# Head norm sums of two attentions, gathered into batches that sit side by side in the columns of the TensorE array

## The chip, the cores and the metric

The kernel runs on one core of one Trainium2 chip, as one program. The metric is the device time of one execution in microseconds (us); lower is better. The core has five engines that matter here, each with its own instruction stream, in order, tied to the others only by semaphores: TensorE (PE, matmuls into the accumulation memory `ps`), VectorE (DVE), ScalarE (ACT), GpSimd (POOL), and SyncE (SP), which issues the DMAs that bring the weights in.

## The reference, cut to what matters

A first block (a state-space mixer, a convolution and a product-key expert layer) is followed by a second block of two transformer layers with four feed-forward parts. The change touches the attention of each of these two layers, and in it the root-mean-square norm of the heads:

```python
def _rms_norm(x, g=None, eps=1e-6):
    y = x * rsqrt(mean(x * x, axis=-1) + eps);  return y * g

# first attention: 8 heads x 2 halves of 64 numbers, for q and for k: 32 sums for each of 272 tokens
q = _rms_norm(q.reshape(bsz, t, 8, 2, 64), qk_norm[0])
k = _rms_norm(k.reshape(bsz, t, 8, 2, 64), qk_norm[1])
...
# second attention: 16 heads of 256 numbers, q alone: 16 sums for each of 256 tokens
q_abs = _rms_norm(q_abs.reshape(bsz, t, 16, 256), q_norm)
```

All data are float32. There are T = 272 tokens (16 of them meta tokens, META; the other 256 are SEQ), the model is D = 1024 = 8 x 128 wide (KD = 8), HEADS = 16, P = 128.

## The kernel before, in words

**Layout and weights.** Activations lie transposed: 128 features on the partitions, the tokens along the free dimension. A weight matrix comes as units of 128 x 1024 float32 (512 KB) into a ring of four slots. For each unit ScalarE makes a high part (`w_hi`, L432), VectorE the rest (`ring_lo`, L438), and TensorE's `split` (L548 to L550) forms the product from three matmuls for each of eight 128 x 128 blocks: high by high, high by low, low by high, so 24 matmuls of 272 columns a unit. A slot is free for the next DMA when TensorE has done its unit (`unit_done`).

**First attention, projection (`a_in`).** Units 0 to 7 give q (two half-heads of 64 rows in each), 8 to 15 give k, 16 to 23 give v. TensorE runs `straight` for unit e; VectorE scales the result out of `ps` (`scale_unit`, L1781) and then makes `ring_lo` of unit e + 2 (`low_ahead`); ScalarE makes `w_hi` of unit e + 2 and then the squares of unit e into `sq[:, e % 8]` (L2307, signal `qk_sq`). The mean over the 64 rows of each half is a matmul: `qk_square_sum(i)` (L919) multiplies the squares of unit i by 32 columns of `pair_mean`, which holds 1/64 in two columns and zeros elsewhere, its window shifted so that the two sums of unit i fall in rows 2i and 2i + 1 of 32 rows of bank 5. The sixteen of them add up in one accumulation. Sum e - 1 follows unit e on TensorE; the last one follows `v_unit(0)`. These are plain float32 matmuls, which the trace records as two passes each.

**What uses the sums.** ScalarE takes the root of the 32 rows (L2310), VectorE the reciprocal (L1856), and `spread_qk(i)` (L945) copies the row pair of unit i out to 128 rows with a matmul against `pair_rows`, 32 rows deep; VectorE's `norm_qk` (L1796) applies it, and the logits follow (`a_logits`, L956).

**Second attention.** Nine units of the up-projection (`up_q(j)`, L1123 to L1125, 256 columns a matmul) give first the index queries and then the sixteen heads, two heads a unit, two 128-row blocks a head. ScalarE squares each block (L2439), GpSimd adds the two blocks of a head (L2611, signal `qa_pair`), and `q_square_sum(hd)` (L1156) sums them with `q_mean` into row hd of bank 4: two after each unit, four after the last. In the same stretch VectorE selects the keys (L1969, L1971: eight rounds of maximum and replace) and makes `ring_lo` of the next units between the rounds. Then ScalarE takes the root (L2460), TensorE turns it (`turn_roots`, L1169), VectorE takes the reciprocal (L1986), and `b_start` uses one column of it for each head.

**Two places whose form is like the change's.** In the state-space mixer of the first block, `mix_step` (L715, L717) makes float32 matmuls of 64 columns whose results go by turns to rows 0 to 63 and 64 to 127 of one bank: for each of four heads two matmuls, so two tiles of the array by turns. In `a_logits` (L956) the two halves m = 0 and m = 1 of a head use rows 0 to 63 and 64 to 127 of the array, each matmul again two passes, and write to two banks.

**The constants.** GpSimd writes `pair_mean`, `q_mean` and `pair_rows` at the start of the first feed-forward part (L2590 to L2599).

Of the kernel before, what the change touches and what calls it, by code (L numbers as in the profile page):

```python
# [14 lines left out]
P = 128  # L15
# [106 lines left out]
def build(nc, a, out):  # L122
# [3 lines left out]
    with ExitStack() as ctx:  # L126
# [209 lines left out]
        meta_t = m3(KD, META)  # L336
        pair_mean = m3(1, 4 * HEADS - 2)[:, 0, :]
        head_mean = m3(1, 2 * KD - 1)[:, 0, :]
        pair_rows = m3(2 * HEADS, 64)
        m3.at = GATED_AT + 2 * (FF_CHUNKS + KD) * T + 2 * KD * 8 + 3 * D  # L340
        q_mean = m3(1, 2 * HEADS - 1)[:, 0, :]
        q_inv = m3(1, SEQ)
# [13 lines left out]
        top8 = m3(1, 16)  # L356
        small_b = m3(1, 64)
        g_b = m3(1, 2)
# [166 lines left out]
        def _(pe):  # L525
# [389 lines left out]

            def qk_square_sum(i):

                pe.wait_ge(qk_sq, i + 1)
                nc.tensor.matmul(ps[0:2 * HEADS, 5, 0:T], pair_mean[:, 2 * (HEADS - 1 - i):2 * (HEADS - 1 - i) + 2 * HEADS],  # L919
                                 sq[:, i % 8, :], start=i == 0, stop=i == HEADS - 1).then_inc(head_stat, 1)  # L920

# [16 lines left out]
            def spread_qk(i):  # L938

                hd, part = i // 2, i % 2  # L940
                if i >= 3:
                    pe.wait_ge(qk_ready, i - 2)
                row = 2 * (KD * part + hd)
                rows = pair_rows[0:2 * HEADS, row:row + 2, :].rearrange("p a n -> p (a n)")
                nc.tensor.matmul(ps[:, 5 + i % 3, 0:T], rows, qk_inv[0:2 * HEADS, 0, :],  # L945
                                 start=True, stop=True).then_inc(head_spread, 1)
# [74 lines left out]
            for e in range(16):  # L1021
                straight("a_in", e, normed(0), T, normed_before=None if e else 8 * NORM["a"])
                if e == 0:
                    summed_stats("a", 0)
                    pe.wait_ge(means_made, 2)
                else:
                    qk_square_sum(e - 1)
            v_unit(0)
            qk_square_sum(15)
            pe.wait_ge(acc_free, OUT0["a_in"] + 15)  # L1030
# [119 lines left out]

            def q_square_sum(hd):

                pe.wait_ge(qa_pair, hd + 1)
                if hd == 0:
                    pe.wait_ge(lat_std, 3)
                nc.tensor.matmul(ps[0:HEADS, 4, 0:SEQ], q_mean[:, HEADS - 1 - hd:2 * HEADS - 1 - hd], sq[:, 2 * hd % 8, 0:SEQ],  # L1156
                                 start=hd == 0, stop=hd == HEADS - 1).then_inc(qa_stat, 1)

            for j in range(2, 10):
                if j < 9:  # L1160
                    up_q(j)
                q_square_sum(2 * (j - 2))
                q_square_sum(2 * (j - 2) + 1)

            def turn_roots():

                pe.wait_ge(head_root, 3)
                for t in range(2):
                    last = nc.tensor.transpose(ps[:, 5, TILE_W + t * HEADS:TILE_W + (t + 1) * HEADS],  # L1169
                                               q_inv[0:HEADS, 0, t * P:(t + 1) * P], ident[0:HEADS, 0:HEADS])  # L1170
                last.then_inc(head_spread, 1)
# [77 lines left out]
        def _(dve):  # L1249
# [605 lines left out]
            dve.wait_ge(head_root, 1)  # L1855
            V_.reciprocal(qk_inv[0:2 * HEADS, 0, :], qk_inv[0:2 * HEADS, 0, :]).then_inc(head_inverse, 1)  # L1856
            scale_unit(17)
# [125 lines left out]
            sb_ = small_b[:, 0, :]  # L1983
            inv = sb_[:, 16:16 + 2 * HEADS]
            dve.wait_ge(head_spread, HEADS + KD + 1)
            link(V_.reciprocal(inv, ps[:, 5, TILE_W:TILE_W + 2 * HEADS]))  # L1986

            def b_start(hd):
                dve.wait_ge(b_logits, hd + 1)
                dve.wait_ge(sel_added, hd + 1)  # L1990
                if hd >= 2:
                    dve.wait_ge(b_turned, 2 * (hd - 1))
                c = 8 * (hd % 2)
                for t, (a0, a1) in enumerate(TILES):
                    ins = V_.scalar_tensor_tensor(soft_b[:, hd % 2, a0:a1], ps[:, hd % 4, a0:a1], inv[:, t * HEADS + hd:t * HEADS + hd + 1],
                                                  bias[:, hd, a0:a1], ALU.mult, ALU.add)
# [35 lines left out]
        def _(act):  # L2032
# [276 lines left out]
            act.wait_ge(head_stat, 16)  # L2309
            A_(qk_inv[0:2 * HEADS, 0, :], ps[0:2 * HEADS, 5, 0:T], ACT.Sqrt, bias=eps[EPS_2][0:2 * HEADS]).then_inc(head_root, 1)  # L2310
            act.wait_ge(lam_mm, 1)
# [147 lines left out]
            act.wait_ge(qa_stat, HEADS)  # L2459
            A_(q_inv[0:HEADS, 0, :], ps[0:HEADS, 4, 0:SEQ], ACT.Sqrt, bias=eps[EPS_2][0:HEADS]).then_inc(head_root, 1)  # L2460
            def value_part(i):
# [53 lines left out]
        def _(pool):  # L2515
# [78 lines left out]
            for half in range(2):  # L2594
                at_col = 2 * (HEADS - 1) + half
                nc.gpsimd.tensor_copy(pair_mean[:, at_col:at_col + 1], C("mean_64")[:, 64 * half:64 * half + 1])
            nc.gpsimd.tensor_copy(pair_rows[0:2 * HEADS, :, :], bc(ident[0:2 * HEADS, 0:2 * HEADS], 2, 64))
            nc.gpsimd.tensor_copy(q_mean[:, HEADS - 1:HEADS], C("mean_256", 1))
            nc.gpsimd.tensor_copy(head_mean[:, KD - 1:KD], C("mean_128", 1)).then_inc(means_made, 1)  # L2599
# [106 lines left out]
```

## Time and profile before

| what | value |
|---|---|
| median of 3 runs | 2277.86 us (2277.47 to 2278.12) |
| span of the profiled execution | 2276.2 us |
| rest of the median beyond that span | 1.66 us |
| PE busy | 2198.8 us (97%) |
| DVE busy | 1609.5 us (71%) |
| ACT busy | 1195.7 us (53%) |
| POOL busy | 319.0 us (14%) |
| DMA, mean over the span | 158 GB/s |

The span runs from the first to the last instruction of one profiled execution; only this span is known of that execution, and the median of the unprofiled runs lies 1.66 us above it. A busy share is an average over stages: 97% says that TensorE nearly always has something in it, not that each of its instructions is on the path that sets the end. Matmul records overlap, since they are pipelined; what a matmul costs is read from the distance between starts, not from its duration.

### The profile page before, as it was taken

To read this page: it belongs to the slowest core of one execution; us is meant where nothing else is said; L and a number is where in the kernel's file an instruction comes from. 1 tells how busy PE (TensorE), PEld (TensorE's weight loads), DVE (VectorE), ACT (ScalarE), POOL (GpSimd) and SP (SyncE) were. 2 spreads that over 40 slices of the span, in tenths; PEclk is the share of its full clock that TensorE was granted. 3 is DMA by queue.
4 is the path that set the end of the run, shared out by engine and by line. 5 is a ranking of instruction groups with operands and counts; after the bars stand their busy time and mean duration, and the time that the engine had idled before them with its cause. 6 is when DMAs were issued, how large, how long until landed. Compare 5 with 4: busy or idle time off the path is not lost.

```text
span 2276.2 us, 42952 instructions
## 1 busy us (share of the span) xinstructions
PE 2198.8 (97%) x15644; PEld 2033.2 (89%) x15644; DVE 1609.5 (71%) x2891; ACT 1195.7 (53%) x1739; POOL 319.0 (14%) x220
## 2 busy tenths in 40 slices
PE   7988999999998999999999999999999999999999
PEld 6986899999997788888899998789999999768998
DVE  6797579999859755555687654667667766866764
ACT  5455357777777655555544443634444434764443
POOL 4785100000007300000011000010000001231000
PEclk9999999999999999999999999889999999999999
DMA  4432556666662366666655554135565556304665
GB/s 160 149 103 84 157 185 185 185 185 185 185 179 100 100 188 187 190 186 189 207 176 173 184 167 117 51 102 173 173 183 180 173 173 191 105 26 139 184 181 179
DMA packets 107976, 359.57 MB, mean 158 GB/s; under 512 B 12992, under 2 KB 21568, under 8 KB 107760
## 3 DMA queue, kind: packets, MB, share of 16 engines
q1 hardware_dynamic: 105792, 354.04, 51.8%
q10 hardware_dynamic: 2096, 4.36, 0.6%
q8 instruction: 55, 0.90, 0.2%
q14 instruction: 33, 0.27, 0.0%
HBM read 356.22 MB, written 6.46 MB: 159 GB/s over the span
## 4 chain that ended last, share of the span: by engine, by line
PE 85%; DVE 8%; ACT 2%; POOL 2%; issue 1%; DMA 1%; SPq 0%; ACTq 0%; DVEq 0%; POOLq 0%
PE ps L548 20%; PE ps L550 19%; PE ps L549 19%; PE ps L854 16%; PE ps L786 3%; DVE hot_keys L1643 2%; DVE big L1652 2%; DVE ring_lo L438 1%; PE ps L1184 1%; POOL ring_lo L438 1%; POOL slot_t L2544 1%; ACT w_hi L432 1%; POOL big L2563 0%; PE ps L919 0%; PE ps L1233 0%
## 5 line engine op out<-in xcount | busy, mean ns | idle before, releaser
L432 ACT ACTIVATE w_hi<-ring 128x1024 fp32r<-128x1024 f32 x640 | 676.1, 1057 | 471.0 <-DMA ring<-in_ffn_in_dram 146.4
L438 DVE TENSOR_TENSOR ring_lo<-ring,w_hi 128x1024 fp32r<-128x1024 f32 x600 | 749.8, 1251 | 232.7 <-ACT w_hi L432 228.6
L548 PE MATMUL ps<-hw_hi,w_hi 128*128 128x272 f32 (+1 forms) x3104 | 893.4, 288 | 11.4 <-DVE ring_lo L438 3.0
L550 PE MATMUL ps<-hw_hi,ring_lo 128*128 128x272 f32 (+1 forms) x3104 | 888.7, 286 | 0.0
L549 PE MATMUL ps<-hw_lo,w_hi 128*128 128x272 f32 (+1 forms) x3104 | 887.1, 286 | 0.0
L548 PEld LDWEIGHTS ps<-hw_hi,w_hi 128*128 128x128 f32 x3104 | 589.0, 190 | 24.8 <-issue 8.8
L550 PEld LDWEIGHTS ps<-hw_hi,ring_lo 128*128 128x128 f32 x3104 | 589.3, 190 | 0.0
L549 PEld LDWEIGHTS ps<-hw_lo,w_hi 128*128 128x128 f32 x3104 | 587.7, 189 | 0.1
L854 PE MATMUL ps<-w_hi,hid_parts 128*128 128x512 f32 x1024 | 279.7, 395 | 2.3 <-DVE hid_parts L1671 2.3
L854 PEld LDWEIGHTS ps<-w_hi,hid_parts 128*128 128x128 f32 x1024 | 192.8, 188 | 47.4 <-issue 2.5
L548 PE MATMUL ps<-gated_hi,w_hi 128*128 128x272 f32 (+1 forms) x704 | 201.7, 287 | 3.6 <-DVE big L1738 3.6
L550 PE MATMUL ps<-gated_hi,ring_lo 128*128 128x272 f32 (+1 forms) x704 | 201.2, 286 | 0.0
L549 PE MATMUL ps<-gated_lo,w_hi 128*128 128x272 f32 (+1 forms) x704 | 200.8, 285 | 0.0
L854 PE MATMUL ps<-ring_lo,hid_parts 128*128 128x512 f32 x512 | 160.5, 394 | 0.0
L1738 DVE TENSOR_TENSOR big<-ps,rstd 128x272 f32<-128x272 f32 (+1 forms) x176 | 76.8, 437 | 109.1 <-PE ps L550 104.4
L2576 POOL TENSOR_TENSOR sq<-sq 128x272 f32<-128x272 f32 (+1 forms) x42 | 48.0, 1142 | 743.7 <-ACT sq L2289 478.4
L548 PEld LDWEIGHTS ps<-gated_hi,w_hi 128*128 128x128 f32 x704 | 132.4, 188 | 4.5 <-issue 4.5
L549 PEld LDWEIGHTS ps<-gated_lo,w_hi 128*128 128x128 f32 x704 | 132.5, 188 | 0.0
L550 PEld LDWEIGHTS ps<-gated_hi,ring_lo 128*128 128x128 f32 x704 | 132.3, 188 | 0.0
L854 PEld LDWEIGHTS ps<-ring_lo,hid_parts 128*128 128x128 f32 x512 | 96.5, 188 | 22.6
L2277 ACT ACTIVATE big<-big 128x272 f32<-128x272 f32 (+1 forms) x88 | 37.7, 429 | 146.7 <-DVE big L1738 146.7
L2232 ACT ACTIVATE hid_parts<-big 128x256 fp32r (+1 forms) x128 | 53.4, 418 | 115.1 <-PE ps L854 111.7
(441 smaller groups left out, 2573.8 us busy)
## 6 DMA issues: line engine op xcount, KB each, us to landing
ring<-in_ffn_in_dram SPq DMA_DIRECT2D x176, 512.0 KB, 3.6
ring<-in_down_dram SPq DMA_DIRECT2D x128, 512.0 KB, 4.2
ring<-in_up_dram SPq DMA_DIRECT2D x128, 512.0 KB, 3.6
ring<-in_ffn_out_dram SPq DMA_DIRECT2D x96, 512.0 KB, 3.7
ring<-in_a_in_dram SPq DMA_DIRECT2D x24, 512.0 KB, 3.6
ring<-in_xbc_dram SPq DMA_DIRECT2D x16, 512.0 KB, 3.6
ring<-in_conf_dram SPq DMA_DIRECT2D x16, 512.0 KB, 3.6
ring<-in_mix_out_dram SPq DMA_DIRECT2D x16, 512.0 KB, 3.6
```

The costliest lines, as they stand in the source:

```text
L432: nc.scalar.activation(w_hi[:, u % RING, :], ring[:, u % RING, :], ACT.Copy).then_inc(hi_done, 1)
L438: eng.tensor_tensor(ring_lo[:, u % RING, :], ring[:, u % RING, :], w_hi[:, u % RING, :].bitcast(F32), ALU.subtract).then_inc(split_done, 1)
L548: nc.tensor.matmul(bank_out, w_hi[:, b, w], hi(k0 + k), start=start and k == 0, stop=False)
L549: nc.tensor.matmul(bank_out, w_hi[:, b, w], lo(k0 + k), start=False, stop=False)
L550: last = nc.tensor.matmul(bank_out, ring_lo[:, b, w], hi(k0 + k), start=False, stop=stop and k == m - 1)
L786: last = nc.tensor.matmul(ps[:, (0, 1, 2, 5)[j % 4], (j // 4) * SEQ:(j // 4 + 1) * SEQ], ring[:, u % RING, k * P:(k + 1) * P], mix[:, KD * ...
L854: last = nc.tensor.matmul(ps[:, 2 * t + half, :], hid_parts[:, part, t * P:(t + 1) * P], weight[:, s, half * 512:(half + 1) * 512], start= ...
L1643: V_.tensor_tensor(hot_b[:, n % 2, :, :].rearrange("p t (a k) -> p t a k", k=8), bc(high_digit[:, at_tok:at_tok + 8, :], 3, 8), bc(gate_lo ...
L1652: V_.tensor_tensor(v, v, ps[:, 2 * b:2 * b + 2, :].rearrange("p c (t i) -> p i (c t)", i=P), ALU.mult).then_inc(gated_hid, 1)
L1738: V_.tensor_tensor((up_a, up_b)[s % 2][:, p, c0:T], ps[:, s, 0:T - c0], rstd[:, c0:T], ALU.mult).then_inc(acc_free, 1)
L2232: A_(hid_parts[:, c % PARTS, :], at(hid, it * 4 + c), ACT.Copy).then_inc(hid_hi_done, 1)
L2576: nc.gpsimd.tensor_tensor(sq[:, 0, c0:T], sq[:, 0, c0:T], sq[:, k, c0:T], ALU.add).then_inc(sq_sum, 1)
```

## The change

In the first attention the sixteen sums are no longer made one at a time. `qk_square_sums(b)` makes four in a row, for units 4b to 4b + 3: the sum of unit 4b + g goes to rows 32g to 32g + 31 of bank 5, which is the column quarter g of the array, and within the quarter to its rows 2b and 2b + 1. The batches follow units 4, 8 and 12 and `v_unit(0)`. Root, reciprocal and `spread_qk` now work on 128 rows, not on 32, and `pair_rows` is laid out for that. In the second attention `q_square_sums(p)` makes the two heads of a unit in a row, the first in quarter 0, the second in quarter 1; root and turning work on 64 and 40 rows, the reciprocal on 80 columns in place of 32. The count of matmuls is the same: 16 and 16. Each still signals its own completion.

```diff
-        pair_mean = m3(1, 4 * HEADS - 2)[:, 0, :]
+        pair_mean = m3(1, 38)[:, 0, :]
...
-        q_mean = m3(1, 2 * HEADS - 1)[:, 0, :]
+        q_mean = m3(1, KD - 1 + 32)[:, 0, :]
...
-        small_b = m3(1, 64)
+        small_b = m3(1, 96)
...
-            def qk_square_sum(i):
-
-                pe.wait_ge(qk_sq, i + 1)
-                nc.tensor.matmul(ps[0:2 * HEADS, 5, 0:T], pair_mean[:, 2 * (HEADS - 1 - i):2 * (HEADS - 1 - i) + 2 * HEADS],
-                                 sq[:, i % 8, :], start=i == 0, stop=i == HEADS - 1).then_inc(head_stat, 1)
+            def qk_square_sums(b):
+
+                pe.wait_ge(qk_sq, 4 * b + 4)
+                for g in range(4):
+                    nc.tensor.matmul(ps[32 * g:32 * g + 32, 5, 0:T], pair_mean[:, 6 - 2 * b:38 - 2 * b], sq[:, (4 * b + g) % 8, :],
+                                     start=b == 0, stop=b == 3).then_inc(head_stat, 1)
...
-                rows = pair_rows[0:2 * HEADS, row:row + 2, :].rearrange("p a n -> p (a n)")
-                nc.tensor.matmul(ps[:, 5 + i % 3, 0:T], rows, qk_inv[0:2 * HEADS, 0, :],
+                rows = pair_rows[:, row:row + 2, :].rearrange("p a n -> p (a n)")
+                nc.tensor.matmul(ps[:, 5 + i % 3, 0:T], rows, qk_inv[:, 0, :],
                                  start=True, stop=True).then_inc(head_spread, 1)
...
-                else:
-                    qk_square_sum(e - 1)
+                elif e % 4 == 0:
+                    qk_square_sums(e // 4 - 1)
             v_unit(0)
-            qk_square_sum(15)
+            qk_square_sums(3)
...
-            def q_square_sum(hd):
-
-                pe.wait_ge(qa_pair, hd + 1)
-                if hd == 0:
+            ROOTS = 32 + KD
+
+            def q_square_sums(p):
+
+                pe.wait_ge(qa_pair, 2 * p + 2)
+                if p == 0:
                     pe.wait_ge(lat_std, 3)
-                nc.tensor.matmul(ps[0:HEADS, 4, 0:SEQ], q_mean[:, HEADS - 1 - hd:2 * HEADS - 1 - hd], sq[:, 2 * hd % 8, 0:SEQ],
-                                 start=hd == 0, stop=hd == HEADS - 1).then_inc(qa_stat, 1)
+                for m in range(2):
+                    nc.tensor.matmul(ps[32 * m:32 * m + 32, 4, 0:SEQ], q_mean[:, KD - 1 - p:KD - 1 - p + 32],
+                                     sq[:, (4 * p + 2 * m) % 8, 0:SEQ], start=p == 0, stop=p == KD - 1).then_inc(qa_stat, 1)
...
-                q_square_sum(2 * (j - 2))
-                q_square_sum(2 * (j - 2) + 1)
+                q_square_sums(j - 2)
...
-                    last = nc.tensor.transpose(ps[:, 5, TILE_W + t * HEADS:TILE_W + (t + 1) * HEADS],
-                                               q_inv[0:HEADS, 0, t * P:(t + 1) * P], ident[0:HEADS, 0:HEADS])
+                    last = nc.tensor.transpose(ps[:, 5, TILE_W + t * ROOTS:TILE_W + (t + 1) * ROOTS],
+                                               q_inv[0:ROOTS, 0, t * P:(t + 1) * P], ident[0:ROOTS, 0:ROOTS])
...
-            V_.reciprocal(qk_inv[0:2 * HEADS, 0, :], qk_inv[0:2 * HEADS, 0, :]).then_inc(head_inverse, 1)
+            V_.reciprocal(qk_inv[:, 0, :], qk_inv[:, 0, :]).then_inc(head_inverse, 1)
...
-            inv = sb_[:, 16:16 + 2 * HEADS]
+            inv = sb_[:, 16:16 + 2 * (32 + KD)]
             dve.wait_ge(head_spread, HEADS + KD + 1)
-            link(V_.reciprocal(inv, ps[:, 5, TILE_W:TILE_W + 2 * HEADS]))
+            link(V_.reciprocal(inv, ps[:, 5, TILE_W:TILE_W + 2 * (32 + KD)]))
...
-            A_(qk_inv[0:2 * HEADS, 0, :], ps[0:2 * HEADS, 5, 0:T], ACT.Sqrt, bias=eps[EPS_2][0:2 * HEADS]).then_inc(head_root, 1)
+            A_(qk_inv[:, 0, :], ps[:, 5, 0:T], ACT.Sqrt, bias=eps[EPS_2]).then_inc(head_root, 1)
...
-            A_(q_inv[0:HEADS, 0, :], ps[0:HEADS, 4, 0:SEQ], ACT.Sqrt, bias=eps[EPS_2][0:HEADS]).then_inc(head_root, 1)
+            A_(q_inv[0:64, 0, :], ps[0:64, 4, 0:SEQ], ACT.Sqrt, bias=eps[EPS_2][0:64]).then_inc(head_root, 1)
...
-                at_col = 2 * (HEADS - 1) + half
+                at_col = 6 + half
                 nc.gpsimd.tensor_copy(pair_mean[:, at_col:at_col + 1], C("mean_64")[:, 64 * half:64 * half + 1])
-            nc.gpsimd.tensor_copy(pair_rows[0:2 * HEADS, :, :], bc(ident[0:2 * HEADS, 0:2 * HEADS], 2, 64))
-            nc.gpsimd.tensor_copy(q_mean[:, HEADS - 1:HEADS], C("mean_256", 1))
+            for b in range(4):
+                quarter = ident.rearrange("p (g r) -> p g r", r=32)[:, :, 2 * b:2 * b + 2]
+                nc.gpsimd.tensor_copy(pair_rows[:, 8 * b:8 * b + 8, :].rearrange("p (g m) n -> p g m n", m=2), bc(quarter, 3, 64))
+            nc.gpsimd.tensor_copy(q_mean[:, KD - 1:KD], C("mean_256", 1))
```

## Rows read from the trace of the kernel before

**Rows 1.** The page: busy time of TensorE, and the chain that ended last.

```profile
PE 2198.8 (97%) x15644; PEld 2033.2 (89%) x15644; DVE 1609.5 (71%) x2891; ACT 1195.7 (53%) x1739; POOL 319.0 (14%) x220
PE 85%; DVE 8%; ACT 2%; POOL 2%; issue 1%; DMA 1%; SPq 0%; ACTq 0%; DVEq 0%; POOLq 0%
```

**Rows 2.** The first attention's sums by their line: durations, first and last start.

```profile
L919 PE MATMUL ps<-sq,big x32: 392/405/418, 1347.2 to 1404.4; 128*32 128x272 f32 x32
```

**Rows 3.** Timeline of TensorE around one sum: start, length, line, count.

```profile
1358.38 0.29 PE L550 MATMUL ps<-hw_hi,ring_lo 128*128 128x272 f32 x1
1358.60 0.65 PE L919 MATMUL ps<-sq,big 128*32 128x272 f32 x2
...
1359.40 0.29 PE L549 MATMUL ps<-hw_lo,w_hi 128*128 128x272 f32 x1
...
1362.18 0.29 PE L550 MATMUL ps<-hw_hi,ring_lo 128*128 128x272 f32 x1
```

**Rows 4.** Timeline of TensorE in the state-space mixer, matmuls of 64 columns.

```profile
147.67 0.45 PE L715 MATMUL ps<-big 128*64 128x128 f32 x4 [1.02 <-POOL big L2563]
...
148.35 0.44 PE L717 MATMUL ps<-big 128*64 128x128 f32 x4
148.72 0.39 PE L548 MATMUL ps<-hw_hi,w_hi 128*128 128x256 f32 x1
```

**Rows 5.** Timeline at the start of the first attention's logits, 0.02 us wide.

```profile
1410.23 0.39 PE L956 MATMUL ps<-big 64*128 64x144 f32 x2
```

**Rows 6.** Timeline of TensorE and VectorE at the start of the projection.

```profile
1345.45 0.29 PE L550 MATMUL ps<-hw_hi,ring_lo 128*128 128x272 f32 x1
1347.22 0.65 PE L919 MATMUL ps<-sq,big 128*32 128x272 f32 x2 [1.48 <-ACT sq L2307]
1347.80 0.39 PE L548 MATMUL ps<-hw_hi,w_hi 128*128 128x272 f32 x1
...
1340.53 2.93 DVE L438 TENSOR_TENSOR ring_lo<-ring,w_hi 128x1024 fp32r<-128x1024 f32 x2
1348.15 1.23 DVE L438 TENSOR_TENSOR ring_lo<-ring,w_hi 128x1024 fp32r<-128x1024 f32 x1 [1.09 <-ACT w_hi L432]
...
1354.92 0.44 DVE L1781 TENSOR_TENSOR big<-ps,rstd 128x272 f32<-128x272 f32 x1 [2.23 <-PE ps L550]
```

**Rows 7.** Timeline of TensorE: a full-width float32 matmul, and the first four spreads.

```profile
1341.92 0.29 PE L550 MATMUL ps<-hw_hi,ring_lo 128*128 128x272 f32 x1
1342.05 0.62 PE L559 MATMUL ps<-sq,con 128*128 128x272 f32 x2
...
1342.68 0.29 PE L549 MATMUL ps<-hw_lo,w_hi 128*128 128x272 f32 x1
...
1407.99 0.29 PE L550 MATMUL ps<-hw_hi,ring_lo 128*128 128x272 f32 x1
1408.21 2.10 PE L945 MATMUL ps<-big 32*128 32x272 f32 x8
```

**Rows 8.** Timeline of TensorE and VectorE in the second attention.

```profile
1963.48 0.28 PE L1125 MATMUL ps<-o_hi,ring_lo 128*128 128x256 f32 x1
1963.69 1.04 PE L1156 MATMUL ps<-sq,big 128*16 128x256 f32 x4
...
1964.88 0.28 PE L1124 MATMUL ps<-o_lo,w_hi 128*128 128x256 f32 x1
...
1982.73 0.38 PE L1123 MATMUL ps<-o_hi,w_hi 128*128 128x256 f32 x1 [0.61 <-DVE ring_lo L438]
...
1997.91 0.78 DVE L1995 SCALAR_TENSOR_TENSOR big<-ps,big 128x144 f32<-128x144 f32 x2 [2.70 <-PE ps L1184]
```

**Rows 9.** Timeline of GpSimd just after the constants.

```profile
1148.06 1.09 POOL L2604 TENSOR_TENSOR big<-big 128x416 f32<-128x416 f32 x1 [10.22 <-DVE gated_lo L1754]
```

**Rows 10.** Stages of the first attention: each engine's busy time, then granted clock, DMA share and GB/s.

```profile
1424.00:1428.00 4.00, 3.94 (x44) 2.75 (x44) 2.30 (x14) 0.36 (x2) 0.00 (x0) 0.50 0.00 0
1480.00:1500.00 20.00, 17.55 (x52) 11.50 (x51) 8.72 (x17) 4.58 (x11) 0.00 (x0) 0.62 0.00 1
```

More of the change, by code:

```diff
@@ L1992, in b_start @@
                     dve.wait_ge(b_turned, 2 * (hd - 1))
-                c = 8 * (hd % 2)
+                c, row = 8 * (hd % 2), 32 * (hd % 2) + hd // 2
                 for t, (a0, a1) in enumerate(TILES):
-                    ins = V_.scalar_tensor_tensor(soft_b[:, hd % 2, a0:a1], ps[:, hd % 4, a0:a1], inv[:, t * HEADS + hd:t * HEADS + hd + 1],
+                    ins = V_.scalar_tensor_tensor(soft_b[:, hd % 2, a0:a1], ps[:, hd % 4, a0:a1], inv[:, row + t * (32 + KD):row + t * (32 + KD) + 1],
                                                   bias[:, hd, a0:a1], ALU.mult, ALU.add)
```

## The prediction

> **What bounds the kernel now.** The page first: TensorE is busy 97% of the span, and 85% of the chain that ended last is its own [rows 1]. So what an edit takes out of TensorE's stream counts at full size, unless another engine paces that stage. The next view is the line of the sums: 32 records for 16 sums of the first attention, from 1347.2 to 1404.4 us [rows 2]. The timeline around one of them gives the price. From the last matmul of a unit (1358.38) to the second of the next (1359.40) are 1.02 us; the steps inside a unit are (1362.18 - 1359.40) / 22 = 0.126 us, so that stretch would be 0.25 without the sum, and the sum costs 0.77 us. The distance from one unit's last matmul to the next one's agrees: 1362.18 - 1358.38 = 3.80 us against 24 x 0.126 = 3.03 [rows 3]. No row there names an idle of TensorE, so TensorE paces the unit, not VectorE (0.44 + 1.23 us a unit, with an idle of 2.23 before it [rows 6]) or a DMA.
>
> The 0.77 us has two parts. Two passes of 272 columns take 2 x 0.23: the first four spreads are 8 passes whose seven distances make 2.10 - 0.39 = 1.71 us [rows 7]. The other 0.31 is the changeover between full-width matmuls and those of 32 columns, paid once on entering and once on leaving. That it belongs to the form is seen on the full-width float32 matmul of the same size, which costs 1342.68 - 1341.92 - 0.25 = 0.51 us [rows 7].
>
> **The change, part by part.**
>
> *Sixteen sums become four batches (first attention).* Removed: 16 x 0.77 = 12.3 us. Added: four batches, each with one changeover (0.31) and four matmuls in four column quarters. No row shows four quarters at once. Bounds from the nearest rows: all four together within one sum's time, 0.77 us; one after another, 0.31 + 4 x 0.46 = 2.15 us; and if each new quarter paid its own changeover, 4 x 0.77 = 3.08 us. The nearest row is the mixer's: 16 records of 128 columns by turns in two column tiles of one bank. A pass of 128 columns is 0.23 x 128 / 272 = 0.108 us, so in sequence they would take 1.73 us. They begin at 147.67, the last group of four ends at 148.79, and the next full-width matmul starts at 148.72, where 0.31 of changeover and tail are still in it: 16 passes in about 0.95 us [rows 4]. So column tiles of float32 overlap, though the later tile's matmuls stand behind the earlier one's two passes in the program. I take 0.80 us a batch, the lower bound and a little for the starts one behind the other, so 3.2 us, and a saving of 9.1 us.
>
> The order in which passes run matters here. At the start of the logits, a window of 0.02 us shows two records that together last only 0.39 us, one record's length, so both started at once; they are the first passes of m = 0 and m = 1, with the first matmul's second pass still to come [rows 5]. "TensorE: Matmul & The Clock Gate" of the Trainium skill, Part 3 ("What overlaps and what doesn't"), says that matmuls start and end in program order, strictly. By the row the batch is one pair of passes; by the rule the quarters would chain, which is a rival below.
>
> *Waits of the batches.* Batch b needs the squares of unit 4b + 3 and follows unit 4b + 4. So its youngest square is one unit back, as for every sum before, and the sum in rows 3 found its square made, with no idle ahead of it: TensorE doesn't wait. The squares' eight buffers: ScalarE needs sum e - 8 before square e; batch 0 (after unit 4) frees 8 to 11, batch 1 (after unit 8) frees 12 to 15. Not late either. Nothing is queued behind these waits that was not before.
>
> *The start of the projection.* Sum 0 followed unit 1 and waited 1.48 us for the first square [rows 6]. Now unit 2 follows at once, at 1345.45 + 0.13 = 1345.58 instead of 1347.80: 2.22 us, of which 0.77 is sum 0, counted above, and 1.45 is new. Its `ring_lo` is there (the pair from 1340.53 ends at 1343.46). What is late next is `ring_lo` of unit 3, which ends at 1348.15 + 1.23 = 1349.38 [rows 6], while unit 2 now ends at 1348.61: TensorE waits 0.8 us. Net 0.65 us. From unit 4 on, `ring_lo` of unit e + 2 is ready some 2.0 us after unit e (an estimate: some 0.35 until scaling starts, 0.44, 1.23 [rows 6]) and is wanted after 3.03, so the faster pace holds, with 1.0 us of slack on VectorE. If that cover were gone, each unit would give back what is missing.
>
> *Spreads with 128 rows.* The passes keep their length. A first spread now starts 0.22 us behind a full-width matmul, not 0.13, and its first step is 1.71 - 6 x 0.23 = 0.33, not 0.23 [rows 7]: about 0.2 us an entry, gone with full rows. There are three entries and one return; those before units whose start waits for other engines give nothing. I take 0.3 us, bounds 0 and 0.8. Root and reciprocal have more partitions but the same length along the free dimension: 0.
>
> *Second attention.* A pair of sums costs 1964.88 - 1963.48 - 2 x 0.118 = 1.16 us [rows 8]; four passes of 256 columns are 0.86 of it. With two quarters at once it is 1.16 - 0.43 + 0.01 = 0.75, 0.41 us less, 3.3 us for eight pairs. But in the middle TensorE waits for VectorE: unit 7 starts after 0.61 us of idle, for its `ring_lo` [rows 8], and the selection rounds that hold VectorE there don't depend on the sums. What is gained before is lost in that wait. Only the pair behind unit 7 counts: 0.4 us; the last four sums wait for GpSimd's last addition, which moves along. Bounds 0 and 0.8. The larger reciprocal lies before an idle of 2.70 us on VectorE [rows 8]: 0. The two turned tiles grow from 16 to 40 rows: under 0.1 us, left out.
>
> *Constants.* GpSimd writes `pair_rows` in four copies in place of one, of the same size per partition in all; behind it lies an idle of 10.22 us [rows 9]: 0. No DMA is added or moved.
>
> *The sum:* 9.1 + 0.65 + 0.3 + 0.4 = 10.45 us. The profiled span 2276.2 becomes 2265.8, and with the 1.66 us by which the median lies above it, 2267.4 us.
>
> **The rivals.**
>
> 1. *The clock moves (0.16).* The granted clock was 0.50 (1.2 GHz) in 1424 to 1428, among the logits behind the last spreads, and 0.62 on average in 1480 to 1500 (so some 15 of 20 us at 1.2 GHz), where the output projection starts [rows 10]. All of this now comes 10 us earlier and with fuller spreads. Work takes twice as long at the lower level, so the 15 us hold up to 7.6 us. If part of it vanishes or as much is added, the result moves by 2 to 4 us either way: 2263.5 or 2270.5.
> 2. *Program order in the array (0.08).* Each quarter's first pass starts with the quarter before's second: 5 x 0.23 + 0.31 = 1.46 us a batch, 5.8 in all; saving 6.5 + 0.65 + 0.3 + 0.2 gives 2270.2. This is what the page's rule above would make of it; rows 5 speak against.
> 3. *Only two quarters at a time (0.05).* 0.31 + 2 x 0.46 = 1.23 us a batch: 2269.2. Rows 4 show two, not four.
> 4. *No overlap of quarters (0.05).* 2.15 us a batch, 8.6 in all: 3.7 + 0.65 + 0.3 = 4.65, so 2273.2, on the edge of what can be told. Rows 4 speak against.
> 5. *Each quarter pays its changeover (0.03).* 16 x 0.77 stay, and the pair on the path of the second attention grows by 0.3: with 0.65 + 0.3 from the rest, 2277.2. Nothing changes; in the mixer there is no room for it.
> 6. *Slower (0.03): the low clock spreads.* If it took hold from the logits on and stayed through the output projection and the feed-forward part behind it, each microsecond at 1.2 GHz costs half of one. It decides from 10.45 / 0.5 = 21 us more at the low level for a tie, and 30 for slower by 0.2%. Against it: those parts run at full pace, and there nothing changes.
>
> **How the numbers follow.** Forecast as worked out: 0.60. Differences within 0.2% (4.6 us) can't be told from none in this kernel. Forecast and rivals 1 to 3 are below 2273.3 (0.89); rival 4 straddles that edge; rival 5 is the same; rival 6 slower. Faster 0.91, same 0.06, slower 0.03. The range takes in rivals 1 to 3 with the bounds of the spreads and the second attention: 2262.5 to 2271.5.
>
> **What the profile would show.** The batches: 16 records from about 1355.5 us, with starts in two clusters 0.23 us apart, and full-width matmuls again about 0.55 us after the first start; 0.80 us against the steps around it. The projection's last sums near 1394.5 rather than 1404.1. An idle of 0.8 us before unit 3, ended by `ring_lo`. No changeover before the spreads. In the second attention unit 7 still starts behind `ring_lo`, its idle longer by 0.4. Wrong would be: batches over 1.2 us, idle between units of the projection, or a low clock in other places than now.

## The result, and the profile after

The changed kernel takes 2261.84 us (median of 4 executions, 2261.41 to 2266.55) against 2277.99 us for the kernel before on the same scale: 16.2 us less. As a ratio it is 0.9927, with a 95% interval of 0.9911 to 0.9942, which is clear of the 0.2% within which the prediction takes two times for the same. The forecast was 2267.4 us in a range of 2262.5 to 2271.5: the direction is right, the gain is larger than forecast, and the time lies 0.7 us below the range. Run again later with more executions, the changed kernel gave 2264.41 us against 2278.82 (ratio 0.9938, 0.9926 to 0.9950). So some 14 to 17 us are gained, where 10.45 were forecast. The kernel before spread over 13 us there (2273.4 to 2286.1 us in 17 executions), which matters for all that follows.

The profiled execution was the one of 2266.55 us, the slowest of its four. The page after, to be read beside [rows 1]:

```profile
span 2264.6 us, 42955 instructions
PE 2187.8 (97%) x15644; PEld 2029.7 (90%) x15644; DVE 1606.0 (71%) x2891; ACT 1195.0 (53%) x1739; POOL 319.9 (14%) x223
```

TensorE has as many matmuls as before and is still 97% busy. The timeline of TensorE around the first batch, to be read beside [rows 3]:

```profile
1355.13 0.29 PE L550 MATMUL ps<-hw_hi,ring_lo 128*128 128x272 f32 x1
1355.35 0.67 PE L920 MATMUL ps<-sq,big 128*32 128x272 f32 x8
1355.95 0.40 PE L548 MATMUL ps<-hw_hi,w_hi 128*128 128x272 f32 x1
1356.18 0.29 PE L549 MATMUL ps<-hw_lo,w_hi 128*128 128x272 f32 x1
```

Eight passes of four sums stand in 0.67 us, where one sum's two stood in 0.65. From the last matmul of the unit to the second of the next are 1.05 us, 0.80 more than two ordinary steps. The line of the sums shows where they end now, beside [rows 2]:

```profile
L920 PE MATMUL ps<-sq,big x32: 392/405/418, 1355.4 to 1394.3; 128*32 128x272 f32 x32
```

And the start of the projection, beside [rows 6]: the wait for the first square is gone, and a shorter one for `ring_lo` of unit 3 has come in its place.

```profile
1348.09 0.29 PE L550 MATMUL ps<-hw_hi,ring_lo 128*128 128x272 f32 x1
1349.14 0.36 PE L548 MATMUL ps<-hw_hi,w_hi 128*128 128x272 f32 x1 [0.77 <-DVE ring_lo L438]
```

Where the time went is read by setting the starts of the same TensorE matmul in both profiles side by side (the n-th matmul of one against the n-th of the other) and taking the difference stage by stage:

| stage, by the times of before | change, us |
|---|---|
| up to the projection of the first attention (1343) | -0.4 |
| the projection with its sums (1343 to 1405) | -9.7 |
| spreads and first logits (1405 to 1434) | -4.5 |
| the heads of the first attention (1434 to 1467) | 0.0 |
| last sums of o and start of the output projection (1467 to 1520) | -3.9 |
| feed-forward parts (1520 to 1933) | 0.0 |
| start of the second attention (1933 to 1962) | +2.4 |
| its up-projection and heads (1962 to 2054) | -0.6 |
| end of its heads, start of its output projection (2054 to 2087) | +5.1 |
| the rest | 0.0 |
| sum (2276.2 to 2264.6) | -11.6 |

The projection does what was forecast. The surprise is in four stages whose instructions hardly changed, and their sum is small in this pair of profiles only because they have both signs. (The low clock that the last of them holds begins a little ahead of 2054; until then the up-projection and its heads were 0.8 us shorter.) The granted clock of a stage shows what it is. Columns of the next fences: stretch in us, its length, each engine's busy time and instruction count (PE, PEld, DVE, ACT, POOL), granted clock, DMA share, GB/s. The first line is spreads and first logits, from the end of the second value unit to the first value product, the second line the last sums of o and the first unit of the output projection. After:

```profile
1395.29:1419.34 24.05, 22.50 (x175) 18.21 (x173) 19.37 (x55) 8.94 (x29) 0.00 (x0) 1.00 0.26 74
1452.53:1480.88 28.35, 24.39 (x92) 14.83 (x91) 13.39 (x27) 11.14 (x30) 0.00 (x0) 0.75 0.00 1
```

The same two stretches of the kernel before (the 20 us in [rows 10] lie inside the second):

```profile
1405.36:1433.94 28.58, 27.02 (x174) 21.63 (x172) 19.47 (x55) 8.83 (x27) 0.00 (x0) 0.82 0.22 60
1467.14:1499.58 32.44, 28.83 (x92) 17.78 (x92) 13.53 (x28) 11.61 (x30) 0.00 (x0) 0.61 0.00 1
```

Spreads and logits ran at the full 2.4 GHz throughout in the one, and at 0.82 in the other, so for a third of the stretch at 1.2 GHz. Was that the change's doing, or did it fall so by chance? One profile of each kernel can't tell.

### The profile page after: what moved, and what is told of

It reads as the page before. It is cut to its first block, busy times and chain, and to the rows that moved or that the text cites. A ratio compares the mean times of both kernels' runs of the same rounds, so it can differ in the third digit from the quotient of the medians.

```text
span 2264.6 us, 42955 instructions
## 1 busy us (share of the span) xinstructions
PE 2187.8 (97%) x15644; PEld 2029.7 (90%) x15644; DVE 1606.0 (71%) x2891; ACT 1195.0 (53%) x1739; POOL 319.9 (14%) x223
## 4 chain that ended last, share of the span: by engine, by line
PE 84%; DVE 8%; ACT 3%; POOL 2%; DMA 2%; issue 1%; SPq 0%; ACTq 0%; DVEq 0%; POOLq 0%
PE ps L548 19%; PE ps L550 19%; PE ps L549 19%; PE ps L854 16%; PE ps L786 3%; DVE hot_keys L1646 2%; DVE big L1655 2%; DVE ring_lo L438 1%; PE ps L1187 1%; POOL ring_lo L438 1%; ACT w_hi L432 1%; POOL slot_t L2547 1%; POOL big L2566 0%; PE ps L1236 0%; PE ps L1237 0%
```

## The experiments

All kernels below ran in three series, each series on one chip and with the kernel before beside them. The theories on the surplus, with the names that they have in the expectations: **A1**, later **R**: it is in the clock of the first attention and comes with the 128-row spreads. **A2**, later **S**: it is in the clock too, but comes because all work arrives earlier, or by chance. (**A** is A1 or A2.) **B**: the second attention's part carries it. The ratio is an estimate of its own, from all executions, and can differ a little from that of the two medians.

| kernel | executions | median us | of before | ratio (95% interval) |
|---|---|---|---|---|
| only the first attention's part | 5 | 2263.96 | 2279.24 | 0.9934 (0.9915 to 0.9954) |
| only the second attention's part | 10 | 2280.22 | 2279.24 | 1.0006 (0.9992 to 1.0020) |
| before, spreads with 128 rows | 11 | 2273.86 | 2279.24 | 0.9967 (0.9953 to 0.9980) |
| before, batches in one quarter | 10 | 2273.00 | 2279.24 | 0.9973 (0.9959 to 0.9987) |
| the changed kernel again | 6 | 2264.41 | 2278.82 | 0.9938 (0.9926 to 0.9950) |
| changed, spreads with 32 rows | 5 | 2265.85 | 2278.82 | 0.9946 (0.9933 to 0.9959) |
| quarters and 128 rows, no batches | 11 | 2271.81 | 2278.82 | 0.9973 (0.9961 to 0.9985) |
| changed, and `spread_o` with 128 rows | 4 | 2258.40 | 2278.82 | 0.9912 (0.9897 to 0.9926) |
| before again | 12 | 2278.62 | 2277.83 | 1.0004 (0.9991 to 1.0017) |
| changed, spreads with 32 rows, again | 6 | 2269.37 | 2277.83 | 0.9960 (0.9945 to 0.9974) |
| before, spreads with 64 rows | 12 | 2275.88 | 2277.83 | 0.9988 (0.9975 to 1.0000) |
| before, `spread_o` with 128 rows | 10 | 2273.02 | 2277.83 | 0.9966 (0.9953 to 0.9980) |

### The two halves of the change

The edits are those of the change, each attention's part alone (in the first: sums, `pair_mean`, `pair_rows`, root, reciprocal, spreads; in the second: sums, `q_mean`, root, turning, the 80 columns).

> Only the first attention's part of the change (batches in quarters, spreads with 128 rows); the second attention as before. The projection should gain 9.9 us in its own stretch, as in the changed kernel. Theory A (the rest of the gain is the clock in the first attention, and comes with this part): 2262.5 us, within 1 us of the changed kernel plus 0.8. Theory B (the second attention's part carries a good share of the surplus): 2266 to 2268.

> Only the second attention's part (two heads in quarters 0 and 1). Theory A: 0.4 to 0.8 us less than before, 2277.2 to 2277.6; low clock in the first attention as before, at 1423 and 1485 us. Theory B: 2272 to 2274.

The first half alone gives 2263.96 us, 15 less than before; the second alone can't be told from no change. Theory B has fallen: what was gained beyond the forecast came with the first half.

### Sums in batches without quarters, quarters without batches

The batch in one quarter is the kernel before with

```diff
-                else:
-                    qk_square_sum(e - 1)
+                elif e % 4 == 0:
+                    for i in range(e - 4, e):
+                        qk_square_sum(i)
...
-            qk_square_sum(15)
+            for i in range(12, 16):
+                qk_square_sum(i)
```

> The kernel before with its sums in batches of four, but all in rows 0 to 31, so one after another in one quarter. A batch should cost 0.31 + 4 x 0.46 = 2.15 us against 0.80 in quarters; the projection saves 3.7 + 0.65 = 4.35 us. If a batch cost 4 x 0.77, the changeover would belong to each sum and not to the stay among full-width matmuls. End: 2273.5 if the clock stays as before (A1); 2269 to 2275 if the earlier arrival alone moves it (A2).

Its timeline around the first batch:

```profile
1358.63 0.29 PE L550 MATMUL ps<-hw_hi,ring_lo 128*128 128x272 f32 x1
1358.84 2.02 PE L919 MATMUL ps<-sq,big 128*32 128x272 f32 x8
1360.79 0.39 PE L548 MATMUL ps<-hw_hi,w_hi 128*128 128x272 f32 x1
1361.03 0.29 PE L549 MATMUL ps<-hw_lo,w_hi 128*128 128x272 f32 x1
```

The same eight passes need 2.02 us in one quarter against 0.67 in four, and the batch costs 1361.03 - 1358.63 - 0.25 = 2.15 us. Its projection was 4.3 us shorter than before, as worked out.

The other one is the first half of the change with one sum after each unit:

```diff
+            def qk_square_sum(i):
+                pe.wait_ge(qk_sq, i + 1)
+                b, g = i // 4, i % 4
+                nc.tensor.matmul(ps[32 * g:32 * g + 32, 5, 0:T], pair_mean[:, 6 - 2 * b:38 - 2 * b], sq[:, i % 8, :],
+                                 start=b == 0, stop=b == 3).then_inc(head_stat, 1)
...
-                elif e % 4 == 0:
-                    qk_square_sums(e // 4 - 1)
+                else:
+                    qk_square_sum(e - 1)
```

> First attention in quarters with 128-row spreads, but one sum after each unit again, so each sum stands alone between full-width matmuls; second attention as before. Each sum should cost 0.77 us as before, so nothing is saved in the projection. Theory R: only the spreads' share, 5 us less than before, as the kernel that had only the 128-row spreads (2274). Theory S: as before, 2279 on this scale.

```profile
1358.12 0.29 PE L550 MATMUL ps<-hw_hi,ring_lo 128*128 128x272 f32 x1
1358.34 0.65 PE L920 MATMUL ps<-sq,big 128*32 128x272 f32 x2
1358.91 0.39 PE L548 MATMUL ps<-hw_hi,w_hi 128*128 128x272 f32 x1
1359.14 0.29 PE L549 MATMUL ps<-hw_lo,w_hi 128*128 128x272 f32 x1
```

A lone sum costs 1.02 - 0.25 = 0.77 us in whichever quarter, and the projection is as long as before within 0.1 us. So the projection's full gain needs both: batches alone save twelve changeovers and the wait at the start (4.3 us), quarters alone nothing, both together 9.7. Yet this kernel, which saves nothing in the projection, is 7 us faster than before. That is the surplus by itself.

### Spreads with more rows

The kernel before, sums one at a time, with

```diff
-                rows = pair_rows[0:2 * HEADS, row:row + 2, :].rearrange("p a n -> p (a n)")
-                nc.tensor.matmul(ps[:, 5 + i % 3, 0:T], rows, qk_inv[0:2 * HEADS, 0, :],
+                rows = pair_rows[:, row:row + 2, :].rearrange("p a n -> p (a n)")
+                nc.tensor.matmul(ps[:, 5 + i % 3, 0:T], rows, qk_inv[:, 0, :],
```

and zeros in the rows of `pair_rows` beyond 32, ones in those of `qk_inv`; the 64-row kernel reads rows 0 to 63 of the same.

> The kernel before with the spreads of the first attention reading 128 rows (the added 96 rows of the pattern are zeros), sums one at a time as before. Theory A1 (full rows keep the clock up from the spreads on): no low clock at 1423 to 1430 us, 4 us or more less, 2270 to 2274. Theory A2 (what counts is that all work comes 10 us earlier, by which the chip's windows fall elsewhere): only the changeovers go, 0.3 us less, 2277.6, low clock at the same times as before.

> As the kernel with 128-row spreads and nothing else changed, but only 64 rows deep. If depth counts by degrees, halfway: 2276 to 2277 against 2279 before and 2274 with 128 rows. If 64 rows are enough: 2274. If they do nothing: 2279, with low clock between 1415 and 1431 us.

With 128 rows the kernel before gains 5.4 us by the medians (4.6 to 10.7 us by the interval of the ratio), with 64 rows 2 us (0 to 5.7). The stretch of spreads and first logits in the profile of the 128-row kernel, then of the 64-row kernel:

```profile
1412.37:1436.41 24.04, 22.49 (x174) 18.19 (x172) 19.38 (x55) 8.83 (x27) 0.00 (x0) 1.00 0.24 72
```

```profile
1402.90:1428.48 25.58, 24.02 (x175) 20.00 (x173) 19.40 (x55) 8.86 (x27) 0.00 (x0) 0.93 0.23 73
```

The first has the length of the changed kernel's, 24.04 against 24.05 us, though nothing before it is faster: arriving earlier isn't needed, and theory A2 has fallen for this stretch. (The profiled execution was the slowest of its kernel, 2287.0 us, but what made it slow lies in other stages.)

### Is the low clock there every time?

> The kernel before once more, for a second profile. If the low clock among spreads and logits belongs to the 32-row spreads, it shows again between 1415 and 1431 us, though its length may differ from the first profile's 10.2 us; if it was chance, it can be missing. Time within 0.1% of the other executions of before.

> The changed kernel once more, for its spread over more executions and a second profile. Theory R (the surplus beyond the sums comes from the 128-row spreads, which keep the clock up among the spreads and logits): 2262 to 2265 us, no low clock between 1400 and 1420 us, in the profile again. Theory S (it was the time of arrival, by chance): low clock there in this profile, and a median of 2265 to 2268.

The kernel before, second profile, in the same two stretches as above:

```profile
1402.90:1433.05 30.15, 28.60 (x174) 23.10 (x172) 19.48 (x55) 8.85 (x27) 0.00 (x0) 0.77 0.20 62
1466.26:1495.60 29.34, 25.38 (x92) 15.13 (x91) 13.31 (x27) 11.37 (x30) 0.00 (x0) 0.71 0.00 1
```

The changed kernel, second profile:

```profile
1396.48:1420.53 24.05, 22.50 (x174) 18.21 (x172) 19.36 (x55) 8.94 (x28) 0.00 (x0) 1.00 0.24 74
1453.73:1483.29 29.56, 25.60 (x91) 15.56 (x91) 13.40 (x27) 11.48 (x30) 0.00 (x0) 0.70 0.00 1
```

Two things are to be seen. The same instructions get another clock in another execution: the first stretch of before took 28.58 and 30.15 us, the second 32.44 and 29.34. And the first stretch sorts by depth all the same. Its length in the profiles so far and those to come: 32 rows, always rows 0 to 31 (before twice, second half alone, batches in one quarter, `spread_o` alone): 28.58, 30.15, 25.94, 25.91, 27.46 us, clock 0.77 to 0.93; 128 rows (six profiles of five kernels): 24.04 to 24.07 us, clock 1.00 each time. The means are 27.6 and 24.05, 3.6 us apart. The one profile with 64 rows (25.58 us, 0.93) lies between.

The second stretch doesn't sort by depth: it is 32.4 us in four profiles, with and without the 128-row spreads, and 28.3 to 29.6 in the eight others that leave `spread_o` as it is, among them one of the kernel before. One thing remains: the six profiles of kernels with sums in quarters in the first attention are all among the short ones, and only two of the six others. So that the 3.9 us there in the table of stages belong to the change isn't shown. Against it stand the clocks of all executions, below, where the kernel with quarters gains nothing over the one that has only the 128-row spreads.

### The changed kernel with 32-row spreads

```diff
-                rows = pair_rows[:, row:row + 2, :].rearrange("p a n -> p (a n)")
-                nc.tensor.matmul(ps[:, 5 + i % 3, 0:T], rows, qk_inv[:, 0, :],
+                p0 = 32 * (hd % 4)
+                rows = pair_rows[p0:p0 + 32, row:row + 2, :].rearrange("p a n -> p (a n)")
+                nc.tensor.matmul(ps[:, 5 + i % 3, 0:T], rows, qk_inv[p0:p0 + 32, 0, :],
```

> The changed kernel with spreads that read only the 32 rows of their unit's quarter, as deep as before the change; sums and batches unchanged. Theory R: the low clock comes back among spreads and logits, some 5 us more than the changed kernel, 2267 to 2270. Theory S: as the changed kernel within 1 us.

> The changed kernel with 32-row spreads (each from its own quarter) once more, since its first profile had no low clock there and its time was 1.4 us above the changed kernel's, too little to tell. Theory R: 2267 to 2270 and low clock at 1405 to 1425 us. Theory R2 (rows 0 to 31 alone for a long time let the clock fall, quarters by turns don't): no low clock there again, 2263 to 2266.

The first profile had no low clock in the stretch, the second had:

```profile
1399.25:1423.52 24.27, 22.20 (x175) 16.88 (x173) 19.19 (x55) 8.94 (x29) 0.00 (x0) 1.00 0.27 71
```

```profile
1394.55:1421.84 27.29, 25.22 (x174) 19.89 (x172) 19.21 (x55) 8.94 (x28) 0.00 (x0) 0.87 0.22 68
```

The first series (2265.85 us) told nothing, and theory R looked wrong; the second (2269.37) is 5 us above the changed kernel. Over both, the mean of 11 executions is 2268.4 us, that of the changed kernel's 10 is 2263.8: with the 128-row spreads taken out and all else kept, 4.6 us are lost. Theory R2, that other quarters by turns suffice, is refuted by the second profile. Root and reciprocal work on 128 rows in this kernel too, so it isn't they that keep the clock up.

### The same at the other thin spread

`spread_o`, which brings the norm of the attention's result to the output projection, reads 8 rows. Here it reads 128, with ones in the added rows of `o_inv` and zeros in those of the identity's column:

```diff
-                nc.tensor.matmul(ps[:, 4 + i % 4, 0:T], ident[0:KD, i:i + 1].broadcast_to([KD, P]), o_inv[0:KD, 0, :],
+                nc.tensor.matmul(ps[:, 4 + i % 4, 0:T], ident[:, i:i + 1].broadcast_to([P, P]), o_inv[:, 0, :],
```

> The changed kernel, and spread_o (L1074, at the start of the output projection) reads 128 rows in place of 8; the added rows meet zeros. Theory R, carried on: the low clock at 1470 to 1483 us goes or shortens, 3 to 7 us less than the changed kernel, 2255 to 2260. Theory S: as the changed kernel within 1 us.

> The kernel before, and only spread_o reads 128 rows in place of 8. On top of the changed kernel this took 6 us; if it is the low clock at the start of the output projection that it removes, it does so here too: 2273, and the second low stretch (17 us long from 1485 us in the first profile of before) is gone.

On the changed kernel it gives 2258.40 us, 6 less than that kernel in the same series; on the kernel before it gives 4.8 less. The stretch of the last sums of o and the first output unit, in the changed kernel with it, then in the kernel before with it:

```profile
1455.76:1479.76 24.00, 20.00 (x92) 12.72 (x91) 13.06 (x28) 11.38 (x30) 0.00 (x0) 0.86 0.00 1
```

```profile
1467.86:1494.48 26.62, 22.97 (x91) 14.67 (x91) 13.10 (x27) 11.60 (x30) 0.00 (x0) 0.74 0.00 1
```

24.00 us against 28.35 and 29.56 in the changed kernel, 26.62 against 32.44 and 29.34 in the kernel before. Over the whole stage (1467 to 1520 in the table of stages) the two are 9.5 and 6.8 us shorter than the first profile of the kernel before, and the other profiles between 4.2 us shorter and 0.1 longer. The fastest kernel of the study is the changed one with this edit, ahead of both kernels of the case: 0.9912 of before, its interval touching that of the changed kernel (0.9926) only at the end.

### The granted clock of every execution

Each execution has its mean granted clock on record, the unprofiled ones too. (1 - clock) times the span is half of the time spent at 1.2 GHz: what the low clock costs, or a little more, since TensorE's waits in that time cost nothing extra. Taken over all executions of a kernel it separates clock from work:

| kernel | executions | mean clock | (1 - clock) x span, us | rest of the span, us |
|---|---|---|---|---|
| before, in all three series | 82 | 0.9870 | 29.6 | 2247.5 |
| before, spreads with 128 rows | 11 | 0.9900 | 22.7 | 2249.2 |
| quarters and 128 rows, no batches | 11 | 0.9903 | 22.1 | 2248.4 |
| before, spreads with 64 rows | 12 | 0.9888 | 25.6 | 2248.0 |
| before, batches in one quarter | 10 | 0.9877 | 28.0 | 2243.7 |
| only the first attention's part | 5 | 0.9898 | 23.1 | 2238.7 |
| only the second attention's part | 10 | 0.9857 | 32.6 | 2245.8 |
| the changed kernel, both times | 10 | 0.9890 | 24.9 | 2237.0 |
| changed, spreads with 32 rows, both times | 11 | 0.9870 | 29.5 | 2236.9 |
| before, `spread_o` with 128 rows | 10 | 0.9897 | 23.4 | 2246.5 |
| changed, and `spread_o` with 128 rows | 4 | 0.9920 | 18.1 | 2238.2 |

A mean over ten executions has a standard error of 1 to 2 us here. The 128-row spreads take 7 us out of the clock's column in the kernel before and none out of the rest; with them taken out of the changed kernel, 4.6 us come back, all in the clock's column. The batches in quarters do the opposite: in the changed kernel with 32-row spreads the rest is 10.6 us less than before and the clock's column is the same. So the surplus is clock, and it follows the spreads in executions that nobody profiled.

## Why the prediction was wrong, point by point

**The step that failed** is "*Spreads with 128 rows*", costed as "I take 0.3 us, bounds 0 and 0.8", together with "The passes keep their length". At the same clock they do, 0.23 us apart with 32 rows and with 128. But the sum took the clock itself as unchanged by the rows, and with 32 rows the stretch had 0.77 to 0.93 of it, with 128 rows all: where it is low, the last spreads of the kernel before start their passes 0.45 us apart (second profile, from 1420.8 us), and the logits behind them stretch likewise. The edit alone is worth 5.4 us (128 rows on the kernel before), 7.0 (quarters without batches, whose projection saves nothing), and 4.6 when taken out of the changed kernel. With 9.7 us in the projection this makes 14 to 17 us, which is what the changed kernel gained in its two series. Rival 1 had named the clock and its end (2263.5), but hung it on the work coming earlier as much as on "fuller spreads", and gave it 0.16 for both signs together. The rows for a better price were at hand: [rows 10] show 1.2 GHz right behind the 32-row spreads, and the edit made those spreads full.

**The batches** were right: 0.80 us each, forecast 0.80; the projection lost 9.67 us, forecast 9.75. The last sums start near 1394.3 (forecast 1394.5). Rivals 2 to 5 are out: they wanted 1.46, 1.23, 2.15 and 3.08 us a batch, and 2.15 is what the kernel with no overlap of quarters showed. Rival 6, slower, didn't come. The count of records was misjudged: a batch has 8 (four sums of two passes), not 16.

**Program order in the array** (rival 2) would have made 1.46 us of a batch. The rule of "TensorE: Matmul & The Clock Gate" of the Trainium skill, Part 3 ("What overlaps and what doesn't"), that matmuls start and end in program order, holds for these only if a float32 matmul counts as one: the four sums start in order and end in order. Pass by pass, as the trace records them, it doesn't: all four first passes start within 0.02 us (from 1355.35), and the four second ones 0.25 us later, so a quarter's first pass doesn't wait for the second one of the quarter before. Only the second passes signal. The same part's span for packed matmuls, one matmul's time plus about 4 ns for each further tile, comes near: 0.65 us for one sum, 0.67 for four side by side.

**The start of the projection** was right: an idle of 0.77 us for `ring_lo` of unit 3, forecast 0.8.

**The changeover before the spreads** went as forecast: the first one starts 0.13 us behind the full-width matmul, and the four are 0.10 us shorter than in [rows 7].

```profile
1397.93 0.29 PE L550 MATMUL ps<-hw_hi,ring_lo 128*128 128x272 f32 x1
1398.06 2.00 PE L946 MATMUL ps<-big 128*128 128x272 f32 x8
```

**The second attention.** A pair costs, beside [rows 8], 1948.35 - 1947.36 - 0.24 = 0.75 us, as forecast, and before unit 7 the idle grew from 0.61 to 1.02 us.

```profile
1947.36 0.28 PE L1126 MATMUL ps<-o_hi,ring_lo 128*128 128x256 f32 x1
1947.57 0.63 PE L1160 MATMUL ps<-sq,big 128*32 128x256 f32 x4
...
1948.35 0.28 PE L1125 MATMUL ps<-o_lo,w_hi 128*128 128x256 f32 x1
...
1966.18 0.38 PE L1124 MATMUL ps<-o_hi,w_hi 128*128 128x256 f32 x1 [1.02 <-DVE ring_lo L438]
```

In this profile the first pair's 0.4 us was kept too (0.8 us by the end of the up-projection, where 0.4 was forecast), since VectorE's first `ring_lo` between the selection rounds took 1.36 us in place of 1.78; why is open. As a whole this half is not to be told from nothing (1.0006), and 0.4 us would be too little to see.

**The other clock shifts of the profile after** are not shown to belong to an edit, nor to belong to none. The end of the second attention's heads grew by 4.3 us at a lower clock, and the second profile of the kernel before grew by 3.1 us at the same place against its first. The same instructions in the first profile of before, in the second, and in the profile after:

```profile
2049.08:2061.75 12.67, 10.43 (x69) 7.44 (x69) 4.31 (x15) 4.26 (x14) 0.00 (x0) 1.00 0.00 1
```

```profile
2044.57:2060.32 15.75, 13.51 (x69) 9.81 (x69) 4.32 (x15) 4.27 (x14) 0.00 (x0) 0.78 0.00 1
```

```profile
2032.13:2049.07 16.94, 14.70 (x68) 9.97 (x68) 4.31 (x15) 4.32 (x14) 0.00 (x0) 0.70 0.00 0
```

All six profiles of kernels with the second attention's part have this low clock, and only three of the eight without it; and the executions show 3 us more in the clock's column with that part alone than before, and 24.9 us in the changed kernel against 22.1 to 23.1 in the three kernels with 128-row spreads and without it. So the second half may well lose in the clock the 0.4 to 0.8 us that it saves, and more. But the differences are no more than twice their error, and the nine profiles with low clock at this place all had some ahead of that half's first sums already (in the profile after, 0.83 from 1930 to 1940 us, the first sum at 1947.57), where its edit can't have brought it. No experiment here separates the two.

Nor does the clock explain why the profiled execution took 5 us more than the changed kernel's other three: its mean clock was 0.989, theirs 0.990, 0.989 and 0.988. That stays open.

**What stays open.** The profiles give the 128-row spreads 3.6 us on average in their own stretch, the times 4.6 to 7.0, and the clocks of all executions 4.6 to 7. So the rest is clock too, but in which stages it lies no profile tells. It is also open what in the spreads counts: with 128 rows both the thin depth and the change of form against the full-width matmuls around are gone. The kernel with 64 rows still has that change (its first spread starts 0.22 us behind a full-width matmul) and has 4 us less in the clock's column, which speaks for the depth, with an error of nearly 2 us.

## What to carry to other kernels

Thin matmuls between full-width ones have two prices, and both are paid by their form: the changeover (0.31 us here), which a batch pays once, and the columns left idle, which four quarters fill at nearly no cost (0.67 us for four sums against 0.65 for one). A matmul that is thin in rows can be filled up with zeros for nothing (its passes are 0.23 us apart either way), and where the granted clock is low in its stretch, try that first: here it was worth 5 us at one place and 5 to 6 at another. Where the clock differs between two executions of the same program, one profile on each side explains nothing; count executions, sort several profiles by the edit in question, and split each execution's time by its mean granted clock.

## What the runs showed of the hardware that was not expected

- The granted clock of the spreads and logits went with the depth of the spreads: 1.00 in all six profiles with 128 rows, 0.93 in the one with 64, 0.77 to 0.93 in five with rows 0 to 31, though TensorE was 94 to 95% busy in all of these. With 32 rows from the four quarters by turns it was 1.00 once and 0.87 once. The output projection's start went from 0.70 and 0.75 to 0.86 when its spreads were filled up.
- The same program got its low clock in other places from one execution to the next: 28.58 and 30.15 us for one stretch, 32.44 and 29.34 for another, and 2272.6 to 2286.7 us in 27 executions of the kernel before.
- Float32 matmuls in four column quarters of one bank ran all at once, though each needs two passes and writes the same columns of the bank, in its own 32 rows: 0.67 us for four, 2.02 us for four in one quarter.
